# A hybrid decoder step on one core: the first token tile's output product gets part of its operands split during the last merge units

## What is computed

```python
merged = jax.nn.sigmoid(ga) * (attn @ p["w_proj_attn"]) + jax.nn.sigmoid(gb) * (h @ p["w_proj_mlstm"])
x = x + merged @ p["w_out"]

xn2 = rmsnorm(x, p["ffn_norm_w"]).reshape(B * T, D_MODEL)
y = x + hier_moe(xn2, p["w_router_group"], p["b_router_group"], ...)
```

## Time and profile before

| | us |
|---|---|
| median of three runs (lowest, highest) | 1524.18 (1521.66, 1528.5) |
| the profiled execution, its own time | 1529.57 |
| span of the profiled execution, first to last instruction | 1527.8 |
| PE busy, share of the span | 1423.3 (93%) |
| DVE busy | 1004.2 (66%) |
| ACT busy | 728.9 (48%) |

### The profile page before, as it was taken

One profiled execution on the slowest core, in us unless ns is written; L12 is line 12 of the kernel. 1 busy time (PEld: TensorE's weight loads), 2 busy tenths in 40 slices (PEclk: granted clock), 3 DMA queues, 4 the chain that ended last, 5 costly groups with the idle time before them and its releaser, 6 DMA issues.

```text
span 1527.8 us, 21515 instructions
## 1 busy us (share of the span) xinstructions
PE 1423.3 (93%) x8013; PEld 1204.5 (79%) x8013; DVE 1004.2 (66%) x1350; ACT 728.9 (48%) x870; POOL 206.1 (13%) x243
## 2 busy tenths in 40 slices
PE   5999999989999998799899969999999999999990
PEld 5999999988999998789788756777777777777760
DVE  3522321156666666766666679888888888888885
ACT  6421121144444445332322227677777777777760
POOL 2600000011111111000100031131111111111014
PEclk8999999999999999999999969999999999999995
DMA  5346323243333322758741089999999999999938
GB/s 195 117 133 215 123 78 69 74 133 102 102 104 125 123 76 61 193 176 231 251 157 48 28 300 367 363 375 394 396 397 395 394 395 392 384 389 393 400 128 321
DMA packets 135895, 347.40 MB, mean 227 GB/s; under 512 B 13768, under 2 KB 92044, under 8 KB 110160
## 3 DMA queue, kind: packets, MB, share of 16 engines
q1 hardware_dynamic: 125672, 312.32, 57.1%
q0 software_dynamic: 6048, 21.50, 4.5%
q10 hardware_dynamic: 4120, 12.85, 2.1%
HBM read 292.34 MB, written 55.28 MB: 228 GB/s over the span
## 4 chain that ended last, share of the span: by engine, by line
PE 44%; DVE 3%; DMA 1%; ACT 1%; issue 1%; POOL 0%; POOLq 0%; ACTq 0%; DVEq 0%
PE xt_ey L2505 4%; PE xt_ey L2506 4%; PE xt_ey L2507 4%; PE y_h_up L2484 4%; PE y_h_up L2483 4%; PE y_h_up L2485 4%; PE logits_gate L2483 2%; PE logits_gate L2484 2%; PE logits_gate L2485 2%; PE ranks_gate L2483 2%; PE ranks_gate L2485 2%; PE ranks_gate L2484 2%; PE y_x L2472 2%; PE y_x L2038 1%; DVE e_w_lo L2364 1%; PE y_x L2039 1%
## 5 line engine op out<-in xcount | busy, mean ns | idle before, releaser
L2364 DVE TENSOR_TENSOR e_w_lo<-mixed,e_w_hi 128x2048 fp32r<-128x2048 f32 x64 | 145.8, 2296 | 2.4 <-ACT e_w_hi L2297 2.3
L2364 DVE TENSOR_TENSOR e_w_lo<-w_out,e_w_hi 128x2048 fp32r<-128x2048 f32 x64 | 143.5, 2283 | 2.9 <-ACT e_w_hi L2297 2.9
L948 PE MATMUL gate_banks<-f_hi,wg_hi 128*128 128x360 f32 (+1 forms) x368 | 125.1, 340 | 1.9 <-PEq L98 1.5
L2297 ACT CAST e_w_hi<-mixed 128x2048 fp32r<-128x2048 f32 x62 | 117.2, 1917 | 15.6 <-ACT e_y_rows L2318 8.9
L2297 ACT CAST e_w_hi<-w_out 128x2048 fp32r<-128x2048 f32 x64 | 121.8, 1904 | 0.6 <-ACT e_y_rows L2318 0.6
L949 PE MATMUL gate_banks<-f_lo,wg_hi 128*128 128x360 f32 (+1 forms) x368 | 121.5, 330 | 0.0
L950 PE MATMUL gate_banks<-f_hi,wg_lo 128*128 128x360 f32 (+1 forms) x368 | 121.3, 330 | 0.0
L2505 PE MATMUL xt_ey<-e_w_hi,e_hT_hi 128*96 128x512 f32 x256 | 103.3, 404 | 4.7 <-DVE e_w_lo L2364 3.6
L2226 POOL CAST idx<-token_of_slot 96x1 uint32 (+1 forms) x30 | 50.3, 1676 | 404.3 <-PE y_x L2472 370.9
L2506 PE MATMUL xt_ey<-e_w_lo,e_hT_hi 128*96 128x512 f32 x256 | 102.1, 399 | 0.0
L2483 PE MATMUL y_h_up<-e_w_hi,e_x_hi 128*96 128x512 f32 x256 | 100.8, 394 | 0.7 <-DVE e_w_lo L2364 0.7
(11 more groups left out here) (616 smaller groups left out, 3619.3 us busy)
## 6 DMA issues: line engine op xcount, KB each, us to landing
w_out<-in_w_down_e SPq DMA_DIRECT2D x64, 1024.0 KB, 8.5
mixed<-in_w_gate_e SPq DMA_DIRECT2D x32, 1024.0 KB, 7.4
mixed<-in_w_up_e SPq DMA_DIRECT2D x32, 1024.0 KB, 8.8
w_gate<-in_w_gate_e SPq DMA_DIRECT2D x32, 1024.0 KB, 7.3
w_up<-in_w_up_e SPq DMA_DIRECT2D x32, 1024.0 KB, 8.3
expert_rows<-e_y_rows ACTq DMA_DIRECT2D x32, 384.0 KB, 7.4
proj<-mixed SPq DMA_DIRECT2D x8, 1408.0 KB, 5.6
w_ring<-in_w_in SPq DMA_DIRECT2D x7, 1408.0 KB, 10.7
```

Of the source, the lines that this page charges most:

```text
L948: pe.matmul(bank, wg_hi[j][:, k, :], hi, start=(k == 0), stop=False)
L2297: act.copy(hi(i, step, j), raw(i, u, j)).then_inc(hi_ready[i], 1)
L2364: dve.tensor_tensor(lo(i, u, j), raw(i, u, j), hi(i, step, j).bitcast(F32), ALU.subtract).then_inc(lo_ready[i], 1)
```

## The change

It does five things.

1. In the merge stage ACT casts tile 0's merged rows (`m0_hi`) behind weight tile 12, and the rows k = 5, 6, 7 of `w_out` at full width behind the weight tiles 13, 14, 15. DVE subtracts `m0_lo` behind weight tile 13 and the three rows behind weight tiles 14 and 15 and behind unit 22.
2. SP issues the loads of the five other rows of `w_out` two units earlier: behind `again(18)` instead of behind `again(20)`, with the wait for `outs` ahead of them. They now stand ahead of the loads of weight tiles 14 and 15.
3. In the route stage ACT and DVE split the five remaining rows, in the order 2, 3, 4, 0, 1, each at full width (128x1024).
4. PE's first product takes the k rows in the order 5, 6, 7, 2, 3, 4, 0, 1, both column halves of a row one after the other, and waits only for the last five.
5. `w_hi`, `w_lo`, `m0_hi` and `m0_lo` get their places before the merge stage, `w_hi` and `w_lo` at the addresses that they had; `m0_hi` and `m0_lo` lie where the route stage keeps its two `xh` tiles.

```diff
+EARLY_K, LATE_K = (5, 6, 7), (2, 3, 4, 0, 1)
...
                 for m in range(FIRST_UNITS + 1, UNITS - 3):
                     again(m)
-                sp.wait_ge(s["outs"], 16 * (3 + 3 * SB))
-                for k in range(5):
-                    load_out(k)
+                    if m == FIRST_UNITS + 2:
+                        sp.wait_ge(s["outs"], 16 * (3 + 3 * SB))
+                        for k in LATE_K:
+                            load_out(k)
...
                 for n in range(9, 2 * KD):
                     w_split(n)
+                    if n == 12:
+                        act.wait_ge(s["outs"], 16 * (3 + 3 * SB))
+                        act.wait_ge(s["merged"], FIRST_UNITS)
+                        act.copy(R.m0_hi[:], merged0[:, 0, :, :]).then_inc(s["m0_hi_ready"], 1)
+                    if n > 12:
+                        k = EARLY_K[n - 13]
+                        act.wait_ge(R.w_out_loaded[k], 16)
+                        act.copy(R.w_out_hi[:, k, :], R.w_out[:, k, :]).then_inc(s["early_hi_ready"], 1)
...
                     n = unit(m)[1] + 2
                     if n < 2 * KD:
                         w_split(n)
+                    if m == UNITS - 5:
+                        dve.wait_ge(s["m0_hi_ready"], 1)
+                        dve.tensor_tensor(R.m0_lo[:], merged0[:, 0, :, :], R.m0_hi[:].bitcast(F32), ALU.subtract)
+                    elif UNITS - 5 < m < UNITS - 1:
+                        i = m - (UNITS - 4)
+                        k = EARLY_K[i]
+                        dve.wait_ge(s["early_hi_ready"], i + 1)
+                        dve.tensor_tensor(R.w_out_lo[:, k, :], R.w_out[:, k, :], R.w_out_hi[:, k, :].bitcast(F32), ALU.subtract)
...
-        for ks in FIRST_K:
-            act.copy(m_hi[0][:, ks, :], merged(0, P)[:, ks, :]).then_inc(s["first_hi_ready"], 1)
-            if ks.start == 0:
-                w_out_hi(0, 0)
-        for k in range(1, KD):
-            w_out_hi(0, k)
-        for k in range(KD):
-            w_out_hi(1, k)
+        for k in LATE_K:
+            act.wait_ge(R.w_out_loaded[k], 16)
+            act.copy(w_hi[:, k, :], w_out[:, k, :]).then_inc(s["w_hi_ready"], 1)
         stationary(1)
...
-        for k in range(1, KD):
-            w_out_lo(0, k)
-        for k in range(KD):
-            w_out_lo(1, k)
+        dve.sem_inc(s["m_ready"], 1)
+        for i, k in enumerate(LATE_K):
+            dve.wait_ge(s["w_hi_ready"], i + 1)
+            dve.tensor_tensor(w_lo[:, k, :], w_out[:, k, :], w_hi[:, k, :].bitcast(F32), ALU.subtract).then_inc(s["w_lo_ready"], 1)
         stationary(1)
...
     def on_tensor(pe):
+        def first_product():
+            for n, k in enumerate(EARLY_K + LATE_K):
+                if k in LATE_K:
+                    pe.wait_ge(s["w_lo_ready"], n - len(EARLY_K) + 1)
+                hi, lo = R.m0_hi[:, k, :], R.m0_lo[:, k, :]
+                for half in range(2):
+                    cols = slice(512 * half, 512 * half + 512)
+                    pe.matmul(Y[0][:, cols], hi, w_hi[:, k, cols], start=(n == 0), stop=False)
+                    pe.matmul(Y[0][:, cols], hi, w_lo[:, k, cols], start=False, stop=False)
+                    ins = pe.matmul(Y[0][:, cols], lo, w_hi[:, k, cols], start=False, stop=(n == KD - 1))
+            ins.then_inc(s["y_full"], 1)
...
-        for half in range(2):
-            product(0, 0, P, half)
+        first_product()
```

More of the change, by code:

```diff
@@ L62 @@
 NL = DM + 1
+ROUTE_COLUMNS = 768
+EARLY_K, LATE_K = (5, 6, 7), (2, 3, 4, 0, 1)
 FIRST_PIECES = 2
@@ L1644, in route @@
                   for i, n in enumerate(("hi", "lo")))
-    w_hi, w_lo = (nc.alloc_sbuf_tensor_at(f"w_out_{n}", [P, KD, D], F32R, offset=o) for n, o in (("hi", R.w_at[1][0]), ("lo", R.w_at[0][2])))
+    w_hi, w_lo = R.w_out_hi, R.w_out_lo
+    assert m_at + 16 * KD * P == R.w_hi_at + 4 * KD * D + 16 * KD * P
     free = lambda i: S["featT"][:, :, (3 + i) * P + TS:(4 + i) * P + TS]
@@ L1713, in route @@
     perm = "(p k) c -> p k c"
-    FIRST_K = (slice(0, 2), slice(2, KD))
     def merged(t, r):
@@ L1814, in exps @@
             act.activation(dm[:r], dm[:r], ACT.Exp).then_inc(s["d_exp_ready"], 1)
-        def w_out_hi(half, k):
-            cols = slice(512 * half, 512 * half + 512)
+        for k in LATE_K:
             act.wait_ge(R.w_out_loaded[k], 16)
-            act.copy(w_hi[:, k, cols], w_out[:, k, cols]).then_inc(s["w_hi_ready"], 1)
-        for ks in FIRST_K:
-            act.copy(m_hi[0][:, ks, :], merged(0, P)[:, ks, :]).then_inc(s["first_hi_ready"], 1)
-            if ks.start == 0:
-                w_out_hi(0, 0)
-        for k in range(1, KD):
-            w_out_hi(0, k)
-        for k in range(KD):
-            w_out_hi(1, k)
+            act.copy(w_hi[:, k, :], w_out[:, k, :]).then_inc(s["w_hi_ready"], 1)
         stationary(1)
@@ L2026, in on_tensor @@
     def on_tensor(pe):
+        def first_product():
[9 more added lines that the diff above has]
+            ins.then_inc(s["y_full"], 1)
         def product(t, u, r, half):
-            first = isinstance(t, int) and t == 0
-            if half == 0 and not first:
+            if half == 0:
                 pe.wait_ge(s["m_ready"], t + 1)
@@ L2032, in product @@
             for k in range(KD):
-                if first:
-                    if half == 0:
-                        pe.wait_ge(s["first_lo_ready" if k < FIRST_K[0].stop else "m_ready"], 1)
-                    pe.wait_ge(s["w_lo_ready"], KD * half + k + 1)
                 hi, lo = m_hi[u][:, k, 0:r], m_lo[u][:, k, 0:r]
@@ L2647, in build @@
                 mix_prompt(nc, a, S)
+            R.w_hi_at = S["bias_at"] + ROUTE_COLUMNS
+            R.w_out_hi, R.w_out_lo = (nc.alloc_sbuf_tensor_at(f"w_out_{n}", [P, KD, D], F32R, offset=o) for n, o in (("hi", R.w_hi_at), ("lo", f_lo_at)))
+            at = R.w_hi_at + 4 * KD * D + 16 * KD * P
+            R.m0_hi, R.m0_lo = (nc.alloc_sbuf_tensor_at(f"first_merged_{n}", [P, KD, P], F32R, offset=at + 4 * KD * P * i) for i, n in ((1, "hi"), (0, "lo")))
             sample_and_merge(nc, a, S, R)
```

5 lines of the change are left out of this document (3 added, 2 removed).

## The result

| | us |
|---|---|
| after, median of 6 runs (lowest, highest) | 1533.36 (1531.54, 1535.81) |
| before, median of 6 runs in turn with them | 1526.12 (1521.66, 1528.5) |
| ratio after / before, 95% interval | 1.0049 [1.0037, 1.0061] |
| the profiled execution after, its own time | 1533.44 |

The account below looks back on a forecast made before the run. The prediction took the expert stage, a stream of weights, as the bound, so earlier shifts count one for one. +4.4 (unit 22) + 1.6 (its clock) - 1.8 (earlier start) - 1.6 (product's clock) = +2.6 us: 1526.8, range 1519.5 to 1532.

Parts of the forecast that it names:

- A: late tile 14: Merge stage: weight tile 14 comes 4.0 us late behind the moved loads, unit 22 loses 4.4 us; 1526.8 us, chance 0.50.
- The stream's part: Merge stage, DMA: the 2.62 MB of moved loads ahead of weight tile 14 end at about 734.2.
- The clock behind the wait: PE at unit 22: one stretch of 3.4 us at 1.2 GHz, costing about 1.6 us.
- Unit 22's wait: Last but one merge unit: PE waits 4.4 us, named after DVE; right if 3 to 6, wrong if under 1.
- `m0_lo` is hidden: Merge stage, DVE: this subtraction delays unit 20's first bank to 729.7, with 0.6 us left, so priced at 0.
- Unit 23 doesn't wait: End of the merge stage: tile 15's DVE chain ends near 744.7, before unit 22 is finished, and costs nothing more.
- the product: Route stage: PE's first product starts with the stage, with no wait for `w_out_lo`, and takes 12.8 us instead of 14.33.
- The early splits alone: Merge and route stages: only the gains are left if the moved loads cost nothing, -3.4 to -4.9 us.
- C: Merge stage: the stream moves at a small-packet mixture's rate, unit 22 10.9 us late; +10.6 us, 1534.8, chance 0.08.
- B: Merge stage: the moved loads cost little or nothing; 1519.3 to 1520.8, or 1523 to 1524.6 with issue slip, chance 0.32.
- What stands ahead in SP's queue is paid: Merge stage, SP's queue: tile 14 waits for all 2.62 MB ahead of it, giving the +2.6 us.
- Mark (5): Route stage from tile 1 on and experts: lengths stay, so the shift of tile 1's first matmul, +2.6 us, is the end's.

Follow-up runs that it names:

- loads_only: The kernel before with only the five `w_out` loads moved ahead of weight tile 14's loads: 1535.49 us, 1.0068 of before.
- loads_back: The changed kernel with the five `w_out` loads issued behind the last merge loads again: 1522.39 us, 0.9984 of before.
- behind_tile: The changed kernel with the five `w_out` loads issued behind weight tile 14's own transfers, ahead of gate pair 22 and tile 15: 1532.55 us, 1.0041 of before.
- c_after: The changed kernel repeated unedited: 1534.08 us, 1.0064 of before.
- after_p4: The changed kernel unedited, one further profiled run: 64.7 us from the sample part's last transposition to tile 1's product.
- after_p3: The changed kernel unedited, one further profiled run: 65.2 us from the sample part's last transposition to tile 1's product.
- early_first: The changed kernel with row 5's subtraction put ahead of weight tile 14's on DVE: 1531.16 us, 1.0033 of before.
- loads_only_order: The kernel before with the five loads moved, in order 2, 3, 4, 0, 1; one run: 67.8 us from the sample part's last transposition to tile 1's product.
- other_queue: The changed kernel with the five `w_out` loads issued by ACT instead of SP: 1531.95 us, 1.0038 of before.

## Why the prediction was wrong

**The cost of tile 14's lateness was mis-sized; that is the step that failed.** "A: late tile 14" was the mechanism: `loads_only` shows it alone, `loads_back` takes it away, `behind_tile` moves it to the next tile. Its size was set by "Then come the 0.52 MB of weight tile 14. At the 301 GB/s at which tile 13 came in the earlier trace rows they take 1.7 us". The stream's part was nearly right: the rate falls from 395 to 208 GB/s at 730 (aligned 734.2, as foretold), though the last row's last packet landed at 731.3. But tile 14 was complete only 3.5 us behind the fall and not 1.7: of the 1.44 MB issued behind it 0.46 MB, 1.4 us, were moved before it was complete, a term that the prediction didn't have, and the small pieces moved at 208 to 309 GB/s. So it was 5.7 us late instead of 4.0 in the profile after. From first issue to cast the prediction had 11.7 us (724.26 to 736.0); the four profiles of after have 13.3, 13.9, 15.8 and 14.7, 14.4 in the mean. These 2.7 us are nearly all of what the stretch lost beyond the forecast (+5.5 against +2.6), and the spread had no place in the range.

**The clock behind the wait.** Expected were 3.4 us at half speed; it was 6.8 us in after, `c_after` and `after_p4` and 10.2 us in `after_p3`. Part of it passes while PE idles, so in after it costs 1.8 us instead of 1.6; it is no large error there.

**Right, by their marks.** Unit 22's wait is named after DVE and the chain from the cast takes 4.12 us (predicted 4.2), of which the row is 1.14 (`early_first`). `m0_lo` is hidden: DVE takes the bank behind it at 725.49, aligned 729.65, where 729.7 was expected. Unit 23 doesn't wait: ACT is ready with tile 15 at 738.3, before unit 22 is half through. The gap is 2.52 us (2.5), the product 12.71 us (12.8) and without a wait for `w_out_lo`. The early splits alone, `loads_back`, were worth -3.4 to -4.9 us by the sum; its stretches are 55.1, 53.1 and 53.4 against 58.0 (-2.9 to -4.9), its medians by the ratios -2.4 and -2.9 us.

**The rivals.** C had the right sign. Its +10.6 is met by single profiles (`loads_only_order`, `loads_only` and `after_p3` come to +9.8, +11.3 and +7.2 in the stretch) and not by the mean of after (+5.5), and it had the wrong reason: the stream of `w_out` was not slowed below 240 GB/s, in after it ran at 330 to 395 from 722 to 730; the small pieces behind it were slow (184 to 309 in the windows from 730 to 738). B is refuted. "What stands ahead in SP's queue is paid" stands (`behind_tile`), but is not the whole: on a queue of their own the same bytes delay the tiles as much (`other_queue`).

**The stages behind, priced at nothing.** Four profiles of after and two of before put the loss in the stretch at 63.5 - 58.0 = +5.5 us; the ratios want +7.5 and +9.8. From tile 1's product to the end after takes 767.1, 765.9, 767.5 and 766.5 us, 766.8 in the mean, and the thirteen profiles of before and of the other kernels 763.5 to 765.6, 764.4 in the mean. So 2.3 us more are lost there, and with them the profiles come to +7.8. They arise behind the last matmul, in the last gathers, where the experts' rows are fetched and added: up to the end of PE's work all seventeen profiles take 727.8 to 728.9 us, and from there to the end after takes 37.5 to 39.3 and the others 34.9 to 37.4. Mark (5) held for the route stage and the experts and failed at the tail. The cause is open and no experiment was made on it: kernels with the same code there, `early_first` and `behind_tile`, have 35.6 and 36.0, and no row names what differs.

**What paces the experts isn't shown by the rates.** "The expert stage is a stream of weights" was read from 363 to 400 GB/s. Its blocks follow each other at 18.02 us in both profiles. From 1000 to 1060 us PE is busy for 59.0 of 60 us in both and the DMA engines' share is 1.00 and 1.01, so either could set the pace. It was without consequence: the blocks keep their length.

## What to carry to other kernels

A prefetch that is issued ahead of a transfer which somebody waits for delays it by all its bytes and by a part of what is queued behind, which varied here from 0.5 to 1.1 MB and spread the delay by 3.6 us; put it behind the last transfer with a deadline, and don't expect another queue to help. Splitting a change into its data moves and its compute moves, one kernel each, told here at once that the compute half gained (0.998) and the data half lost more (1.007). For a change of a few us, take several profiles of one kernel before reading a difference between two: the same stretch of the same kernel varied by 4 us.
